# Two-layer trunk with mLSTM, attention and short conv: mLSTM output-gate panels issued in parts, another order of value tiles, other banks in attention

## The reference

```python
for layer in range(DEPTH):                      # DEPTH = 2
    need_ctx = layer < DEPTH - 1                # context outputs are needed in layer 0 only
    p_l = split_columns(modulate(rms_norm(x, norm1[layer]), sh1, sc1) @ w_in[layer])
    p_c = split_columns(modulate(rms_norm(ctx, norm1[layer]), csh1, csc1) @ w_in[layer])
    hm_l, hm_c = mlstm_bidirectional(mq_l, mk_l, mv_l, mg_l, mq_c, mk_c, mv_c, mg_c)   # 4 heads, 2 directions
    ym_l = mlstm_output(hm_l, p_l[3], mlstm_norm[layer])     # rms norm of h, times gain, times sigmoid(o gate)
    ya_l = latent_attention(aq_l, concat([ak_c, ak_l]), concat([av_c, av_l]))          # 8 heads, 2 kv heads, softmax
    ...
```

## Time and profile before

| | |
|---|---|
| median of 3 runs | 1948.4 us (1947.9 to 1950.41) |
| the profiled execution, its own time | 1943.74 us |
| its span, first to last instruction | 1941.9 us |
| TensorE busy | 1872.9 us (96% of the span) |
| DVE / POOL / ACT busy | 979.1 / 729.6 / 689.9 us |
| mean granted TensorE clock | 0.986 |

### The profile page before, as it was taken

The page is one execution under the profiler, slowest core; times in us unless marked ns, Lnnn a source line. Parts: engine busy times, 40 slices in busy tenths (PEclk is TensorE's granted clock), DMA queues, the critical chain, the costliest instruction groups (busy, mean ns, idle before and its releaser), DMA issues.

```text
span 1941.9 us, 27168 instructions
## 1 busy us (share of the span) xinstructions
PE 1872.9 (96%) x11175; PEld 1607.7 (83%) x11175; DVE 979.1 (50%) x1372; ACT 689.9 (36%) x946; POOL 729.6 (38%) x513
## 2 busy tenths in 40 slices
PE   5999899999999999999999999999999999979998
PEld 3697688778878788778877778799997999969997
DVE  4454543645433443366443544644657656547554
ACT  3333532433222232243232222433543444434443
POOL 2332231112543344544222322432332566746553
PEclk7999999999999999999999999999999999989999
DMA  9221122122444334465225337222232355565562
GB/s 315 66 88 44 44 66 73 58 65 66 150 132 130 111 127 147 135 197 169 91 90 184 107 118 240 81 94 88 66 122 97 109 181 189 174 195 173 177 191 91
DMA packets 240858, 244.64 MB, mean 126 GB/s; under 512 B 6020, under 2 KB 239840, under 8 KB 240736
## 3 DMA queue, kind: packets, MB, share of 16 engines
q1 hardware_dynamic: 240432, 242.80, 39.5%
q10 hardware_dynamic: 304, 0.10, 0.0%
HBM read 241.83 MB, written 1.05 MB: 125 GB/s over the span
## 4 chain that ended last, share of the span: by engine, by line
PE 89%; DVE 4%; SPq 2%; issue 1%; ACT 1%; DMA 1%; POOL 1%; DVEq 0%; ACTq 0%; POOLq 0%
PE pp L931 19%; PE pp L935 19%; PE pp L932 19%; PE pp L939 4%; PE pp L938 4%; PE pp L940 4%; PE pc L1099 3%; PE pp L913 2%; PE pp L915 2%; PE pp L914 2%; SPq L827 2%; PE pc L1020 2%; PE pc L1151 1%; PE pc L1189 1%; DVE wL L1605 1%
## 5 line engine op out<-in xcount | busy, mean ns | idle before, releaser
L1492 POOL TENSOR_TENSOR wL<-raw,wH 128x512 fp32r<-128x512 f32 x360 | 580.2, 1632 | 854.4 <-ACT wH L1203 854.3
L931 PE MATMUL pp<-hH,wH 128*128 128x512 f32 (+1 forms) x1760 | 590.5, 346 | 19.3 <-ACT hH L1388 14.3
L1605 DVE TENSOR_TENSOR wL<-raw,wH 128x512 fp32r<-128x512 f32 x360 | 459.2, 1299 | 266.4 <-ACT wH L1203 261.0
L932 PE MATMUL pp<-hH,wL 128*128 128x512 f32 (+1 forms) x1760 | 582.1, 341 | 0.0
L1203 ACT ACTIVATE wH<-raw 128x1024 fp32r<-128x1024 f32 x360 | 360.3, 1049 | 336.0 <-PE pp L940 222.1
L935 PE MATMUL pp<-hL,wH 128*128 128x512 f32 (+1 forms) x1760 | 457.2, 341 | 2.6 <-POOL hL L1543 1.7
L931 PEld LDWEIGHTS pp<-hH,wH 128*128 128x128 f32 x1760 | 335.6, 191 | 66.8 <-issue 17.8
L932 PEld LDWEIGHTS pp<-hH,wL 128*128 128x128 f32 x1760 | 336.0, 191 | 37.1 <-issue 1.0
L935 PEld LDWEIGHTS pp<-hL,wH 128*128 128x128 f32 x1760 | 304.7, 191 | 44.2 <-POOL hL L1543 6.6
L938 PE MATMUL pp<-yH,wH 128*128 128x512 f32 (+1 forms) x448 | 150.6, 336 | 0.0
L939 PE MATMUL pp<-yL,wH 128*128 128x512 f32 (+1 forms) x448 | 150.6, 336 | 0.0
(11 more groups left out here) (228 smaller groups left out, 2097.3 us busy)
## 6 DMA issues: line engine op xcount, KB each, us to landing
raw<-in_w_in SPq DMA_DIRECT2D x84, 1024.0 KB, 5.2
raw<-in_w_up SPq DMA_DIRECT2D x32, 1024.0 KB, 5.6
raw<-in_w_down SPq DMA_DIRECT2D x32, 1024.0 KB, 5.2
ada_T<-in_w_ada SPq DMA_DIRECT2D x18, 1024.0 KB, 7.9
ada_G<-in_w_ada SPq DMA_DIRECT2D x12, 1024.0 KB, 8.5
ada_Y<-in_w_ada SPq DMA_DIRECT2D x10, 1024.0 KB, 13.0
ada_H<-in_w_ada SPq DMA_DIRECT2D x8, 1024.0 KB, 9.2
raw<-in_w_proj_m SPq DMA_DIRECT2D x8, 1024.0 KB, 5.2
```

Of the source, the lines that this page charges most:

```text
L931: pe.matmul(dsts[b], wh[b], hi[:, kt, ts_], start=first, stop=False)
L932: pe.matmul(dsts[b], wl[b], hi[:, kt, ts_], start=False, stop=False)
L1492: pool.tensor_tensor(wL[:, p % RAW, ks, :], raw[:, p % RAW, ks, :], wH[:, p % HIGH, ks, :].bitcast(F32), ALU.subtract).then_inc(wL_ready, 1)
L1605: dve.tensor_tensor(wL[:, p % RAW, ks, :], raw[:, p % RAW, ks, :], wH[:, p % HIGH, ks, :].bitcast(F32), ALU.subtract).then_inc(wLv_ready, 1)
```

## The change

Four edits. (1) A step kind `part` issues a range of a panel's k-tiles; the old `head` becomes a case of it. In mLSTM the panel `mo` is issued as k-tiles 0 and 1 after the first scores, 2 to 5 after the remaining scores, and 6 and 7 after `value`. On ScalarE, DVE and POOL the whole step of the panel (split of p+2, then `tanh`) stands where the last part stands, behind `value`; `part` has nothing for them. (2) `weigh` is cut in two on TensorE: the scores of key tiles 2 and 3 move to `weigh_late`. (3) `value` computes tiles 2, 3, 0, 1 in layer 0, and all that counts tiles follows. (4) In attention `scores` stands ahead of `qss` and `qrot` in the first two iterations, and layer 1's `probs` use banks 2 and 3 instead of 0 and 1.

```diff
+def spans_tt(l):
+    late = list(range(CTX // P, TT))
+    return late + list(range(CTX // P)) if l < DEPTH - 1 else late
...
         for h in range(MH):
             step("weigh", l, h=h)
+            part("mo", l, h, 0, 0, 2)
+            step("weigh_late", l, h=h)
             if h:
                 step("norm_h", l, h=h - 1)
-            panel("mo", l, h)
+            part("mo", l, h, 0, 2, 6)
             if h:
                 step("turn", l, h=h - 1)
             step("value", l, h=h)
+            panel("mo", l, h)
...
             if 1 <= i <= AH:
                 step("probs", l, h=i - 1)
+            if i < AH:
+                step("scores", l, h=i)
             if i < 2:
                 step("qss", l, j=3 + i)
                 step("qrot", l, j=3 + i)
-            if i < AH:
-                step("scores", l, h=i)
...
         elif k in ("scores", "probs"):
             for b in range(3 if st["l"] < DEPTH - 1 else 2):
-                use(st, b, b)
+                use(st, b, b if k == "scores" or st["l"] < DEPTH - 1 else 2 + b)
```

More of the change, by code:

```diff
@@ L205, in ada_end, with part @@
             step(k, 0, g=g)
+    def part(kind, l, c, b, a, e):
+        panel(kind, l, c, b, k="part")
+        plan[-1]["kts"] = (a, e)
     def heads(l, n):
         for kind, c, b in ((("mk", 0, 0), ("mk", 1, 0)) if n == 1 else (("up", 0, 0), ("up", 1, 0))):
-            panel(kind, l, c, b, k="head")
+            part(kind, l, c, b, 0, KH)
     def spread_apply(l, n, fill=0):
@@ L366, in make_plan @@
     for i, st in enumerate(plan):
-        if st["k"] == "head":
+        if st["k"] == "part":
             q = next(q for q in plan[i:] if q["k"] == "panel" and all(q[n] == st[n] for n in ("kind", "l", "c", "b")))
-            st["p"], q["headed"] = q["p"], True
+            st["p"], q["begun"] = q["p"], st["kts"][1]
     def use(st, name, bank):
@@ L426, in make_plan @@
                 st["u"]["m1"], st["u"]["s1"] = st["u"]["m0"], st["u"]["s0"]
+            weigh_use = st["u"]
         elif k == "value":
-            for tt in range(TT) if st["l"] < DEPTH - 1 else range(CTX // P, TT):
+            for tt in spans_tt(st["l"]):
                 for d in range(2):
@@ L442, in make_plan @@
             use(st, 0, 2)
+        elif k == "weigh_late":
+            st["u"] = weigh_use
         elif k in ("scores", "probs"):
             for b in range(3 if st["l"] < DEPTH - 1 else 2):
-                use(st, b, b)
+                use(st, b, b if k == "scores" or st["l"] < DEPTH - 1 else 2 + b)
         elif k == "attend":
@@ L796, in trunk @@
         dchain = sem("vector_chain")
-        def spans_tt(l):
-            return list(range(TT)) if l < DEPTH - 1 else list(range(CTX // P, TT))
         def norm_cols(st):
@@ L946, in _ @@
                 k, l, u = st["k"], st["l"], st["u"]
-                if k == "head":
-                    run_panel(st, slice(0, KH))
+                if k == "part":
+                    run_panel(st, slice(*st["kts"]))
                 elif k == "panel":
-                    run_panel(st, slice(KH if "headed" in st else 0, KT))
+                    run_panel(st, slice(st["begun"] if "begun" in st else 0, KT))
                 elif k == "start":
@@ L1080, in _ @@
                             filled(last, u[f"s{s}"])
+                elif k == "weigh_late":
+                    h = st["h"]
                     b = claim(u["s2"])
@@ L1092, in _ @@
                     pe.wait_ge(vones, l + 1)
-                    for tt in sorted({key[0] for key in u}):
+                    for tt in spans_tt(l):
                         for d in range(2):
@@ L1426, in _ @@
                         act.wait_ge(hraw_ready, h_count(l, h, tt))
-                        if tt > tts[0]:
-                            act.wait_ge(hss_ready, h_count(l, h, tt - 1))
+                        if tt != tts[0]:
+                            act.wait_ge(hss_ready, h_count(l, h, tt) - 1)
                         act.activation(junk[:, :], hM[:, h, tt, :], ACT.Square, accum_out=mss[:, tt:tt + 1]).then_inc(hss_ready, 1)
@@ L1431, in _ @@
                         continue
-                    act.wait_ge(hss_ready, h_count(l, h, TT - 1))
-                    act.activation(mrs[:, tts[0]:TT], mss[:, tts[0]:TT], ACT.Sqrt, scale=1.0 / MV, bias=eps).then_inc(mrs_ready, 1)
+                    act.wait_ge(hss_ready, h_count(l, h, tts[-1]))
+                    act.activation(mrs[:, min(tts):TT], mss[:, min(tts):TT], ACT.Sqrt, scale=1.0 / MV, bias=eps).then_inc(mrs_ready, 1)
                 elif k == "turn":
@@ L1925, in _ @@
                     dve.wait_ge(mrs_ready, l * MH + h + 1)
-                    rs = mrs[:, tts[0]:TT]
+                    rs = mrs[:, min(tts):TT]
                     link(dve.reciprocal(rs, rs))
@@ L1929, in _ @@
                         i = dve.tensor_scalar(hM[:, h, tt, :], hM[:, h, tt, :], mrs[:, tt:tt + 1], None, ALU.mult)
-                        if tt < TT - 1:
+                        if tt != tts[-1]:
                             start_link(i)
@@ L2024, in h_count @@
     n = [TT if q < DEPTH - 1 else TT - CTX // P for q in range(DEPTH)]
-    first = TT - n[l]
-    return sum(n[q] * MH for q in range(l)) + n[l] * h + tt - first + 1
+    return sum(n[q] * MH for q in range(l)) + n[l] * h + spans_tt(l).index(tt) + 1
 def p_count(l, h):
```

## The result

The changed kernel takes 1956.8 us (median of 5 runs, 1953.62 to 1957.57), the kernel before in the same session 1950.41 (5 runs, 1947.9 to 1951.38): a ratio of 1.0033, 95% interval 1.0019 to 1.0048. Slower by 0.33%, inside the range, 2.6 us under the forecast. The profiled execution of after is 1957.57 us with a span of 1955.8, that of before 1943.74 with 1941.9. The spans differ by 13.9 us where the medians differ by 6.4: the runs of the kernel before lie near 1943.4, 1948 and 1950.7 us, with dips of TensorE's clock that come in one run and not in another (run e12), and its profile is from the lowest. So the trace is read by stage.

A forecast was written before the change was run, and what follows sets the result against it. TensorE, busy for 96% of the span, was taken as the bound. Terms -3.6 + 5.7 + 5.3 + 2.75 + 1.8 - 0.9 = +11.0 us, added to 1948.4, gave 1959.4 us, 0.6% slower; range 1951.5 to 1967.

The forecast's parts named there:

- mLSTM, layer 0: Layer 0's heads, timed from V, the start of `value`: ScalarE's chain sets 26.2 us a head instead of 26.96; sum -3.6 us.
- From their start to the end of the masks: Layer 0's mLSTM: 10.4 us from the exponentials' start to the masks' end, so `value` no earlier than V+26.2.
- mLSTM, layer 1: Layer 1's heads: TensorE has no wait to win and pays ScalarE's chain, 2.1 us a head twice; sum +5.7 us.
- Attention, layer 0: Rotary product waits for bank 2 behind the exponentials: +5.3 and +2.75 us in iterations 0 and 1, +1.8 for clock.
- I add +1.8 once: Layer 0's attention: lower TensorE clock behind the 6.6 us idle stretch, charged once at +1.8 us.
- nothing to 1.8 us each, taken as nothing: Clock loss behind the shorter 2.4 us waits of attention iteration 1 and layer 1's heads, taken as zero.
- Rival (c): The 2.5 us waits in layer 1's heads and iteration 1 lower the clock too: four times 1.8, 1966 us; chance 0.12.
- Attention, layer 1: Scores' 4.0 us of waits go, `probs` costs +1.8, the first two iterations +1.3; sum -0.9 us, bounds -4 and +3.
- between 0 and 3 us, I take +1.3: Layer 1's attention, first two iterations: `qss` and `qrot` wait for DVE to empty banks 3 and 2 of `probs`.
- (a): mLSTM: ScalarE in time, heads run at TensorE's pace, -7 and -1 us instead of -3.6 and +5.7; 1949.3 us; chance 0.07.
- (b): TensorE sets the pace in mLSTM, and layer 0's rotary product finds bank 2 free: -13.3 us, 1935; chance 0.05.
- Rival (d): Table loads ahead of the exponentials on ScalarE cost twice their length, another 1.28 us each: +7.7, 1967.1 us; chance 0.04.

The follow-up runs named there:

- e12: The kernel before, unchanged, run and profiled a second time; its profiled run took 1947.61 us.
- e4: The kernel after with the split of panel p+2 issued at the second part of `mo` instead of its last; 1954.56 us, ratio 1.0037.
- e5: The mLSTM edits alone (attention of before), with `value` put back behind the whole panel `mo`; 1947.29 us, ratio 1.0006.
- e6: The mLSTM edits alone (attention of before), with layer 0's value tiles in the old order; 1947.43 us, ratio 1.0003.
- e9: e5 with the late scores put back directly behind the first ones; 1949.21 us, ratio 1.0017.
- e8: The kernel after with 18 and 6 unread matmuls filling TensorE's idle time in layer 0's attention, iterations 0 and 1; 1952.09 us, ratio 1.0033.
- e7: The kernel after with only head 0's scores put back behind `qss` and `qrot`; 1950.8 us, ratio 1.002.
- e11: e10 plus banks 2 and 3 for the transposed softmax of heads 1 to 7 in layer 1's attention; 1933.65 us, ratio 0.9935.
- e10: Layer 0's mLSTM as after with early split, layer 1's with `value` behind the panel and late scores, attention of before; 1936.85 us, ratio 0.9952.
- e2: The kernel before with the attention edit alone; 1957.88 us, ratio 1.006.
- e1: The kernel after with the attention of before, so the mLSTM edits alone; 1947.95 us, ratio 1.001.

## Why the prediction was right

**mLSTM, layer 0: -5.6 for -3.6.** The mechanism is as described: squares, split, load, `tanh`, then `EP` at V+15.5 (predicted V+15.8), first `value` 2.7 us earlier (14.30 to 11.60, predicted 2.7), +1.5 behind the last head (predicted 1.4). What failed is "From their start to the end of the masks the trace has 10.4 us ..., and `value` cannot start earlier": in after it is 9.45 (209.60 to 219.05), as the masks took 2.21 us and not 3.12. That term was the duration of an operation in company, and I moved it without its company; 0.9 in each of the two later steps, and some 0.35 in the first (24.51 us, predicted 24.9). With masks that short, the "wait for POOL's masks" ahead of `value` did not come either: what TensorE waits for, 0.41 us, is the scaled `hM` ahead of `turn`, as in layer 1, and the masks end while `turn` runs. In heads 1 to 3 the masks take 3.11 or 3.12 where VectorE's half of a split (1.47 us) lies beside them (before, e4, e5), and 2.21 where it does not (after, e6). Within one set in before, a single mask takes 0.29 to 0.34 us, and 0.74 beside the subtraction. No run was made for that alone.

**mLSTM, layer 1: +5.2 for +5.7.** Heads 16.94 us apart (17.1), the first step 15.67 against 15.06 (+0.6, predicted 0.8), first `value` -0.9 (predicted -0.7), the end +1.6 (predicted 1.4). "In layer 1's mLSTM no wait of that kind shows" was wrong: the wait of the second scores stood on the weight loads, 0.5 us in three heads (e5, e9), and the earlier trace rows shows TensorE's matmuls alone.

**Attention, layer 0: +11.9 for +9.85.** The idle terms were right: from the scores' start to the next panel it takes 345.35 - 333.56 = 11.79 us in e8, predicted 11.9, and both blocks together cost 7.7 us at full clock, predicted 8.05. The step that failed is the clock: "I add +1.8 once" (the loss worked out from the earlier trace rows was 1.6, and no row gives 1.8), and "nothing to 1.8 us each, taken as nothing" for the shorter wait. It came behind both, 4.1 us together (e8). The second block alone costs 4.2 us (e7, predicted 2.75), the first the other 7.7 (predicted 7.1 with its clock). Rival (c) had put a dip behind the shorter wait, and in layer 1's heads too, where none came: TensorE waits 0.8, 2.1 and 2.1 us ahead of `turn` there, and the clock stayed full.

**Attention, layer 1: +0.3 for -0.9.** The small sum hides two errors that nearly cancel. The "+1.8" for `probs` behind `attend` in bank 3 is right: 1.9 us in seven places, on the weight loads, in after as in e11. The gain on the scores was taken too small: the earlier trace rows has TensorE's matmuls alone, and the weight loads of the same line waited as well. Before:

```profile
PEld pc L1151 <- DVE prT L2004: 1.9, 7, 0.4
```

From e10 to e11 both rows together fall from 7.3 to 1.4 us, and 5.9 gained less 1.9 paid is the 4.0 by which the stages differ. The first two iterations, "between 0 and 3 us, I take +1.3", cost 151.29 - 146.85 = 4.4 us, beyond the upper bound; 2.6 of it is one wait for VectorE's copy out of bank 3 and some of the rest a clock of 0.57 from 1472 to 1480 us. Price and place of the first were named, its dip was not; and since e12 shows dips in this stage behind waits that e10 has without one, it is not shown that this wait brought it.

**Parts: 0 for 0.** e9 has layer 1 at 59.16 us with the panels cut in three, as before: no cost for changing between fp32 and fp32r more often.

**Sum.** The four stages that the edits touch add up to +11.8 us (predicted +11.0), the medians to +6.4, with an interval of 3.7 to 9.4. Some of this closeness is luck: in the stages, 2.0 and 0.5 us too much in the mLSTM stand against 2.05 and 1.2 too little in attention; and the time of 1956.8 lies 2.6 us from the forecast because a change forecast 4.6 us too large was added to a median of before (1948.4) that five runs then put 2.0 us higher. e2, with the attention edit alone, stands 11.0 us above its runs of before (7.6 to 15.8 by its interval), and e1 1.1 above them. The five runs of before beside the result had a median of 1950.41, the 81 later ones medians of 1945.9 to 1947.6; against those the 1956.8 us would be a loss of 9 to 11 us, which is nearer to the stages' sum. The profile of before is also faster than all five of those runs, and that of after is the slowest of its own five. How much of the difference is the small sample and how much the session stays open. Rivals (a) and (b), with ScalarE in time, fell: `EP` starts directly behind `sig_o` in every head that I read, at V+15.46 in layer 0 and V+9.8 in layer 1 (predicted 15.8 and 10.0). Rival (d) fell too: `tanh` at 208.38 starts 0.01 us behind the load's end and the load 0.02 behind the split, as in the earlier trace rows. The drain of about 1380 ns that the Trainium skill, page ScalarE: Activation LUTs, section What ACT_TABLE_LOAD costs, puts beside the load shows in no run read here.

## What to carry to other kernels

A step moved earlier on the busiest engine is moved earlier on all of them: look at what then stands in front of the next link of the chain on the in-order engines, and move that too (e4), or leave the step where the engine had nothing to win (layer 1). Before a product is put behind others that share its PSUM bank, follow who gives the bank back, here VectorE behind ScalarE's exponentials; give other banks only to those uses that have no neighbour waiting behind (e11). Judge each edit by its stage and layer: taken together this change lost 0.3%, and its winning parts, with the split moved early, gain 0.65%.

## What the runs showed of the hardware

- During a wait of 2.40 us or directly behind it TensorE's clock fell in all four profiles that have it in layer 0's attention (after, e2, e4, e7; some 3.4 us at the lower level in e7), but not behind 2.34 us that followed filling work (e8), nor behind waits of 2.1 us in layer 1's mLSTM. In layer 1's attention waits of 1.2 and 2.1 us have a dip behind them in one profile and none in another (before, e12, e10). 4.1 us of clock came back with 24 matmuls whose results nobody reads.
- Dips in unchanged code come in one run and not in another (the window 852 to 858 us: 1.00 and 0.73), and the runs of one kernel lie in groups 2.5 to 5 us apart. That the dips alone make the groups is read from two profiles and not shown.
- GpSimd's eight masks of 128x128 take 2.21 us, and 3.12 with an fp32r subtraction of VectorE beside them; that subtraction (two of 128x512) takes 1.47 us beside the masks in before and e4, and 2.75 us in after, where GpSimd's part of the same split runs beside it. With nothing of GpSimd beside it one of the two takes 0.68 us (e6). No run was made to take them apart:

```profile
206.96 2.75 DVE L1621 TENSOR_TENSOR wL<-raw,wH 128x512 fp32r<-128x512 f32 x2
```

- A matmul's wait for its bank can be booked on the weight load: a view of TensorE's waits on PE alone missed 1.6 us in three places of layer 1's mLSTM, and in its attention 1.9 us in seven before and another 1.9 us in seven after.
